# Two-layer decoder trunk in fp32: where the first modulation sums, the forget gate and the clearing products stand in the order

## What is computed

```
mod = silu(c) @ ada_w[l] + ada_b[l]            # shift, scale, gate for attention and experts
h   = x * (1 + sc_a) + sh_a
q, k, v = split(h @ fox_w_in);  logf = log_sigmoid(h @ w_f + b_f)      # the forget gate
o   = softmax(q k^T / 8 + cum(logf)_i - cum(logf)_j, causal) v
x   = layer_norm(ALPHA * x + (1 + g_a) * (o @ w_o))
h   = x * (1 + sc_f) + sh_f
probs = softmax(h @ router_w);  pick best group, then its top 2;  gates = probs / their sum
m   = sum_e gates[:, e] * ((silu(h @ w_gate[e]) * (h @ w_up[e])) @ w_down[e])
x   = layer_norm(ALPHA * x + (1 + g_f) * m)
```

## Time and profile before

| what | value |
|---|---|
| median of 3 runs | 953.62 us (953.47 to 956.13) |
| profiled execution, its own time | 949.71 us |
| its span, first to last instruction | 948.0 us |
| mean granted TensorE clock | 0.978 |
| TensorE busy | 869.6 us, 92% of the span |
| VectorE busy | 370.2 us, 39% |
| ScalarE busy | 168.0 us, 18% |
| GpSimdE busy | 69.7 us, 7% |
| HBM read | 302.49 MB |

### The profile page before, as it was taken

One profiled execution on the slowest core, in us unless ns is written; L12 is line 12 of the kernel. 1 busy time (PEld: TensorE's weight loads), 2 busy tenths in 40 slices (PEclk: granted clock), 3 DMA queues, 4 the chain that ended last, 5 costly groups with the idle time before them and its releaser, 6 DMA issues.

```text
span 948.0 us, 11352 instructions
## 1 busy us (share of the span) xinstructions
PE 869.6 (92%) x3720; PEld 404.5 (43%) x3721; DVE 370.2 (39%) x918; ACT 168.0 (18%) x373; POOL 69.7 (7%) x110
## 2 busy tenths in 40 slices
PE   6897999989999899899979999997999989889985
PEld 3673665434333333233348467543333333333331
DVE  2285667475122221121148687566222212212215
ACT  1101233011111111111110125410211111101020
POOL 1000000040000000000030000213000000000000
PEclk9999999998999999999989999998999999999998
DMA  9999672857699999679993998240199999959911
GB/s 359 432 421 428 277 321 90 355 206 326 242 430 428 427 429 429 271 322 431 425 428 143 375 418 338 89 156 22 66 431 429 427 427 430 429 209 428 428 60 44
DMA packets 23359, 303.95 MB, mean 321 GB/s; under 512 B 2720, under 2 KB 3232, under 8 KB 5280
## 3 DMA queue, kind: packets, MB, share of 16 engines
q1 hardware_dynamic: 22752, 303.14, 76.5%
q10 hardware_dynamic: 576, 0.40, 0.1%
HBM read 302.49 MB, written 1.05 MB: 320 GB/s over the span
## 4 chain that ended last, share of the span: by engine, by line
PE 79%; DMA 9%; DVE 7%; issue 2%; ACT 1%; POOL 0%; SPq 0%; DVEq 0%; ACTq 0%
PE ps L1654 23%; PE ps L1662 10%; DMA ring<-in_moe_w_up_dram 8%; PE ps L1667 7%; PE ps L1461 6%; PE ps L1474 6%; PE ps L1490 6%; PE ps L1572 5%; PE ps L1636 3%; PE ps L1718 1%; PE ps L1629 1%; PE ps L1391 1%; DMA ring<-in_ada_w_dram 1%; PE ps L1523 1%; PE ps L1426 1%
## 5 line engine op out<-in xcount | busy, mean ns | idle before, releaser
L1654 PE MATMUL ps<-ring,hT 128*64 128x512 f32 x560 | 251.4, 600 | 17.7 <-DMA ring<-in_moe_w_up_dram 9.3
L1655 PE MATMUL ps<-ring,hT 128*64 128x512 f32 x560 | 251.8, 601 | 0.0
L1654 PEld LDWEIGHTS ps<-ring,hT 128*64 128x64 f32 x560 | 74.8, 138 | 173.2 <-issue 173.2
L1663 PE MATMUL ps<-ring,arena 128*64 128x512 f32 x256 | 116.7, 599 | 0.0
L1662 PE MATMUL ps<-ring,arena 128*64 128x512 f32 x256 | 116.7, 598 | 0.0
L1173 DVE TENSOR_TENSOR arena<-arena,ps 128x256 f32<-128x256 f32 x32 | 13.5, 421 | 240.8 <-ACT arena L752 132.1
L387 DVE SCALAR_TENSOR_TENSOR acc<-ring,csig,acc 128x512 f32<-128x512 f32 x112 | 84.2, 752 | 3.9
L1655 PEld LDWEIGHTS ps<-ring,hT 128*64 128x64 f32 x560 | 74.8, 138 | 0.0
L1667 PE MATMUL ps<-arena 128*128 128x512 f32 x144 | 66.6, 605 | 3.2 <-DVE arena L1182 3.2
L1182 DVE TENSOR_TENSOR arena<-ps,gbc 64x512 f32<-64x512 f32 x70 | 48.0, 686 | 42.6 <-PE ps L1663 41.5
L1461 PE MATMUL ps<-hT,ring 128*128 128x256 f32 x256 | 58.3, 392 | 3.4 <-issue 1.9
(11 more groups left out here) (262 smaller groups left out, 938.2 us busy)
## 6 DMA issues: line engine op xcount, KB each, us to landing
ring<-in_moe_w_gate_dram SPq DMA_DIRECT2D x32, 2048.0 KB, 12.4
ring<-in_moe_w_up_dram SPq DMA_DIRECT2D x32, 2048.0 KB, 16.0
ring<-in_moe_w_down_dram SPq DMA_DIRECT2D x32, 2048.0 KB, 17.2
ring<-in_ada_w_dram SPq DMA_DIRECT2D x24, 2048.0 KB, 16.0
ring<-in_fox_w_in_dram SPq DMA_DIRECT2D x6, 2048.0 KB, 11.0
ring<-in_kv_ada_w_dram SPq DMA_DIRECT2D x4, 2048.0 KB, 12.6
ring<-in_kv_w_dram SPq DMA_DIRECT2D x4, 2048.0 KB, 19.3
ring<-in_fox_w_o_dram SPq DMA_DIRECT2D x2, 2048.0 KB, 13.2
```

Of the source, the lines that this page charges most:

```text
L1654: t.matmul(ps[0:CAP, bank, :], lhs(k), wcols(ng)[:, k, :], start=(k == 0), stop=(k == KC - 1))
L1655: mm = t.matmul(ps[CAP:P, bank, :], lhs(k), wcols(nu)[:, k, :], start=(k == 0), stop=(k == KC - 1))
L1663: mm = t.matmul(ps[CAP:P, bank, :], lhs(f), wdown(n)[:, f, 512:D], start=(f == 0), stop=(f == 3))
```

## The change

In layer 0's value projection, VectorE copies the first modulation sums and makes `share(2, 0)` before it does the forget gate's five operations, and does `mod_cols(1)` and `gate_row(0)` after unit 11's copy instead of ahead of `share(2, 1)`. TensorE does the second value piece straight after `mod_sum(1)`, and `turn_mod(1, 4)` and `spread_gate(0, 5)` behind it. In the routing, four clearings are added ahead of the wait for the mask in layer 0, and eight stand there in layer 1 instead of three; behind it there are two instead of three in both layers.

```diff
@@ VectorE, layer 0 projections
                 if u == GATE_UNIT + 1:
-                    forget_gate()
                     mod_rows(1)
                 if u in (1, 3, 5, 7):
                     share(1, u // 2)
                 if u == GATE_UNIT + 1:
                     share(2, 0)
+                    forget_gate()
                 if u == GATE_UNIT + 2:
-                    mod_cols(1, 4)
-                    gate_row(0, 5)
                     share(2, 1)
+            mod_cols(1, 4)
+            gate_row(0, 5)
             share(2, 2)
@@ TensorE, route(l)
                 if l == 0:
                     mod_product(4, range(4, KC))
+                    zeroed((6, 7, 6, 7))
                 else:
-                    zeroed((0, 0, 0))
+                    zeroed((0, 6, 7, 0, 6, 7, 0, 6))
                 residual(l, 1)
                 pe.wait_ge(rt_mask, l + 1)
...
                 pe.wait_ge(tot_r, l + 1)
-                zeroed((1, 1, 1))
+                zeroed((1, 1))
@@ TensorE, layer 0 projections
             mod_sum(1)
+            natural_units(u, N_V[0][1:])
             turn_mod(1, 4)
             spread_gate(0, 5)
-            natural_units(u, N_V[0][1:])
             query_unit(0, 0, hT)
```

## The result

The changed kernel took 940.37 us in the median of 4 runs (939.09 to 942.44), against 953.59 us (953.47 to 956.13). The ratio is 0.9857 with a 95% interval of 0.9831 to 0.9884. Two later comparisons of the same pair, on other occasions, gave 0.9901 (0.9885 to 0.9917) and 0.9875 (0.9839 to 0.9910). The forecast's ratio was 0.9887.

The account below looks back on a forecast made before the run. It took TensorE to bound the kernel, 79% of the last chain, losing time standing still or at half clock. -5.0 - 2.8 - 3.0 = -10.8 us, from 953.62 to 942.8 us, range 940.5 to 947.0.

Parts of the forecast that it names:

- the last of the sum: Whole kernel: the median lies 5.6 us above the profiled span, carried over, so 953.62 - 10.8 = 942.8 us.
- The row weighed against the rule: Profile windows 120 to 122: clock stayed at 1.00 through a 2.27 us wait, set against the skill's rule of repeated throttling.
- The new wait: Value projection, TensorE ahead of unit 12, for the forget gate's bank: 2.5 us in place of 5.95 us.
- Part A: Layer 0's value projection, reordered: query units start at 97.3 instead of 102.38, rounded to -5.0 us.
- Part B: Both routings, clearings changed: the gather starts earlier, -2.8 us in layer 0 and -3.0 us in layer 1.
- the far bound: Routings: VectorE's copy of the totals comes 1.0 us earlier, giving -3.1 us in layer 0 and -3.3 in layer 1.
- That it reaches the end: Experts: weight queues are empty before the first round and the stream moves with TensorE, so every microsecond counts once.
- The clock in the new wait: Rival, value projection: the clock falls and unit 12 starts at half clock; -9.1 us, 944.5; chance 0.18.
- VectorE did not eat anything: Rival: VectorE's 1.8 us cover before the first scores is misjudged by 4 us; -8.3 us, 945.3; chance 0.09.
- The clearings held the clock: Rival, routings, claimed the opposite: clearings do not hold the clock, gain there only 3.2 us; sum -8.2, 945.4; chance 0.10.
- The transfers took nothing back: Rival, experts, claimed the opposite: the stream of weights takes all back; no change, 953.6 us; chance 0.04.
- The slower case: Rival, routings: the clock has already fallen when clearings start, each takes 1.71 us; total +5.1, 958.7 us; chance 0.04.

Follow-up runs that it names:

- again_before: The kernel before the change, unchanged, profiled and timed again: 956.98 us in the median of 12 runs, ratio 1.0001 to itself.
- half_filled: The changed kernel with two and five clearings ahead of the masks instead of four and eight: 948.78 us, 0.9933 of the kernel before.
- behind_only: The changed kernel without the clearings added ahead of the mask's wait, with two behind it: 948.97 us, 0.9915 of the kernel before.
- warm_start: The changed kernel with three filling products more in the first modulation: 942.62 us, 0.9855 of the kernel before.

## Why the prediction was wrong, point by point

**The step that failed** is the last of the sum: "The median lies 5.6 us above the span, and I carry the difference over." That takes the clock falls of one profiled execution, and the distance between it and its median, for a property of the kernel. The repeats show that they are a draw. Over 14 profiles of all versions, first key product to first query has a clock fall near 34 us in 7 of the 12 that lack the fills, worth 1.4 to 3.0 us. The 2.3 us wait near 120 had a fall in 11 of the 12 that have it; the one without was the first profile of before, worth 1.6 us. First expert product of layer 1 to the end takes 274.0 to 274.3 us in four, and 276 to 279 in the others (274.0 before, 277.8 in `again_before`). The first profile of before had drawn the short end of all three. Its own median lay 3.9 us above its time, that of after 1.3 above. So the medians of the first comparison moved by 13.2 us while the profiles moved by 10.6. The offset between time and median thus shrank by 2.6 us, and the range had left 1.4 us below the forecast's own spread for it. The mean of the three ratios is 0.9878, against the forecast's 0.9887; the gap to the range was 0.13 us, well inside the draw. The two later medians, 946.77 and 942.89 us, lie inside the range, so the miss by 0.13 us has luck in it as well.

**The row weighed against the rule** was that same lucky row: the clock at 1.00 through 2.27 us. In 11 of 12 profiles that wait did cost the clock, and 2.42 us in `half_filled` did too, so the row was no ground for expecting the clock to hold through 2.5 us. The new wait came out shorter, at 1.86 us, and there the clock held in 6 of 8. The Trainium skill, in "TensorE: Matmul & The Clock Gate", section "HAM oscillation — how this bites in real kernels", tells of waits for transfers of some 3 to 5 us between short bursts, each of which throttles TensorE again. The prediction applied that to a wait of 2.5 us, shorter than those of the page. The traces here agree with the page at 3.1 us and more, and show falls at shorter waits as well.

**Part A** was right in mechanism and size. First key product to first query went from 67.49 to 62.31 us, 5.2 against my 5.0, counted against the first profile of before. The new wait was 1.86 us, not 2.5. VectorE's chain from the sum to the gate's end was 0.2 us shorter than I had added up, and the trace counts unit 11 until its last product has drained, 0.4 us later than I did.

**Part B** was right in both layers: strip sum to gather fell by 2.88 and 3.12 us against -2.8 and -3.0. The layer 0 figure is again that of the first profile: against `again_before` the gain there is 1.7 us. The value taken near the far bound was the right one, and the four narrow products came down to 0.8 us from 1.73.

**That it reaches the end** was right. Before the first experts' round both kernels have the same 15.7 to 15.8 us from gather to first expert product, and the 10.6 us of the span are there at the end, with the additions and losses elsewhere that the section on the result names.

**The rivals.** The clock in the new wait is real, in 2 of 8 profiles, at 1.7 us. VectorE did not eat anything. The price of that rival was a little high: a cover of 1.8 us misjudged by 4 leaves 2.8 of the 5.0, not 2.5. The clearings held the clock, and the changed kernel against `behind_only` shows it (13.33 and 13.19 us against 15.24 and 14.96). The transfers took nothing back. The slower case did not come: the clock stood at 1.00 when the clearings began in every profile that has them.

## What to carry to other kernels

Where an engine's clock depends on its waits, one profile is one draw: take two or three of the kernel before and compare stretch by stretch before adding a profile's difference to a median. A wait is worth its length plus what its fall costs behind it (here 1.6 to 1.7 us for one in attention, 1.9 for the part of the routing behind the mask), so filling it with idle products can pay even where no work can be moved. It did in the routing (1.9 and 1.8 us); at the start (`warm_start`) the stretch got its full clock, but no gain in time could be seen. When a step is moved behind another engine's long operation, look for the latest point at which the moved step is still free: splitting the share at its third strip gave the gate its place and took the new wait away.

## What the runs showed of the hardware

The same program on one chip took 953.2 to 958.7 us over 23 runs, and the mean granted clock (0.975 to 0.966) follows the time, with small exceptions. Products of ones with zeros held the clock at 1.00: in the nine profiles with four and eight clearings ahead of the masks, no fall stands between the strips' sum and the gather. The wait of 1.57 us in `half_filled` did not cost the clock in its one profile, that of 1.86 us did in 2 of 8, that of 2.3 us in 11 of 12, and the waits of 3.1 us and more ahead of the masks did in all four profiles that have them.

Those are single places, and length alone does not decide. I took all waits of TensorE from 1.4 to 4.2 us, later than 25 us from the start, in the 14 profiles, without those that began at half clock, and counted where the clock fell during the wait or within 2 us behind it. From 1.4 to 1.65 us it was 9 of 95, seven of them at the keys' start near 34 us. From 1.65 to 2.2 us it was 43 of 87, from 2.2 to 2.5 us 12 of 13, from 2.6 to 3.0 us 32 of 43, and for the eight waits ahead of the masks all. One wait of 2.86 us in the first profile, in the experts of layer 1, did not cost the clock.
